# One trunk kernel: the score sweep on row tiles, with unpadded queries, and output squares read from PSUM

## The reference, cut to what matters

```python
rel = b[:, :, :, :, None, :] - b[:, :, :, None, :, :]        # b: cumulated log decay
pair_decay = jnp.exp(jnp.minimum(rel, 0.0)) * causal[:, :, None]
scores = jnp.einsum('bhnid,bhnjd,bhnijd->bhnij', qc, kc, pair_decay)
o_intra = jnp.einsum('bhnij,bhnjv->bhniv', scores, vc)
...
o = rms_norm(o, out_norm) * jax.nn.silu(r.reshape(B, S, H, GLA_DV))
```

## Time and profile before

| | us |
|---|---|
| median of three runs (1468.25 to 1469.93) | 1468.33 |
| the profiled execution | 1469.45 |
| its span | 1467.7 |
| PE busy | 1432.9 (98%) |
| weight loads busy | 1175.7 (80%) |
| DVE, ACT, POOL busy | 727.6, 618.6, 651.1 |
| mean granted TensorE clock | 0.994 |

### The profile page before, as it was taken

One profiled execution on the slowest core, in us unless ns is written; L12 is line 12 of the kernel. 1 busy time (PEld: TensorE's weight loads), 2 busy tenths in 40 slices (PEclk: granted clock), 3 DMA queues, 4 the chain that ended last, 5 costly groups with the idle time before them and its releaser, 6 DMA issues.

```text
span 1467.7 us, 17267 instructions
## 1 busy us (share of the span) xinstructions
PE 1432.9 (98%) x6777; PEld 1175.7 (80%) x6777; DVE 727.6 (50%) x1122; ACT 618.6 (42%) x1073; POOL 651.1 (44%) x369
## 2 busy tenths in 40 slices
PE   8999989999999999999999999999999999999999
PEld 6878778886888888888878776878867888888887
DVE  6473585244566404663135645843536663166621
ACT  5646572465432212232246455735644322222221
POOL 4646253452344434444346354624524344444442
PEclk9999999999999999999999999999999999999999
DMA  6322002331233232332333310123312333333322
GB/s 166 105 88 71 16 3 88 99 114 58 75 98 102 92 108 87 102 99 94 88 86 91 97 59 15 50 66 101 110 48 83 105 90 104 93 100 90 107 85 93
DMA packets 174208, 125.66 MB, mean 86 GB/s; under 512 B 12561, under 2 KB 150576, under 8 KB 174128
## 3 DMA queue, kind: packets, MB, share of 16 engines
q1 hardware_dynamic: 173568, 124.55, 28.3%
q10 hardware_dynamic: 560, 0.01, 0.0%
HBM read 122.44 MB, written 2.10 MB: 85 GB/s over the span
## 4 chain that ended last, share of the span: by engine, by line
PE 91%; DVE 5%; ACT 2%; POOL 1%; issue 1%; DMA 1%; SPq 0%; DVEq 0%
PE bank L608 26%; PE bank L610 26%; PE bank L609 26%; PE bank L871 3%; PE bank L718 1%; PE bank L616 1%; PE bank L830 1%; PE bank L831 1%; PE bank L706 1%; DVE h L1494 1%; ACT cprobs L1084 1%; DMA h<-in_x 1%; POOL scores_h L473 1%; DVE state L1666 1%; PE bank L775 0%
## 5 line engine op out<-in xcount | busy, mean ns | idle before, releaser
L535 POOL TENSOR_TENSOR w_lo<-raw,w_hi 128x1024 fp32r<-128x1024 f32 (+1 forms) x230 | 543.6, 2367 | 735.1 <-ACT w_hi L1045 735.0
L1045 ACT ACTIVATE w_hi<-raw 128x1024 fp32r<-128x1024 f32 (+1 forms) x230 | 237.6, 1036 | 337.1 <-PE bank L610 333.6
L608 PE MATMUL bank<-x_hi,w_hi 128*128 128x512 f32 (+1 forms) x880 | 345.0, 392 | 0.7 <-issue 0.7
L609 PE MATMUL bank<-x_lo,w_hi 128*128 128x512 f32 (+1 forms) x880 | 342.9, 390 | 0.0
L610 PE MATMUL bank<-x_hi,w_lo 128*128 128x512 f32 (+1 forms) x880 | 342.9, 390 | 0.0
L608 PEld LDWEIGHTS bank<-x_hi,w_hi 128*128 128x128 f32 (+1 forms) x880 | 165.0, 187 | 38.1 <-issue 3.4
L609 PEld LDWEIGHTS bank<-x_lo,w_hi 128*128 128x128 f32 (+1 forms) x880 | 164.9, 187 | 35.3 <-issue 0.8
L610 PEld LDWEIGHTS bank<-x_hi,w_lo 128*128 128x128 f32 (+1 forms) x880 | 164.8, 187 | 35.4
L1494 DVE TENSOR_TENSOR h<-h,bank 128x512 f32<-128x512 f32 x64 | 43.7, 688 | 223.9 <-PE bank L610 223.9
L608 PE MATMUL bank<-w_hi,a_hi 128*128 128x512 f32 x352 | 137.0, 389 | 0.0
L610 PE MATMUL bank<-w_hi,a_lo 128*128 128x512 f32 x352 | 136.9, 389 | 0.0
(11 more groups left out here) (288 smaller groups left out, 2100.2 us busy)
## 6 DMA issues: line engine op xcount, KB each, us to landing
raw<-in_w_ffn_in SPq DMA_DIRECT2D x88, 512.0 KB, 3.8
raw<-in_w_ffn_out SPq DMA_DIRECT2D x40, 512.0 KB, 3.7
raw<-in_w_in SPq DMA_DIRECT2D x28, 512.0 KB, 3.8
raw<-in_w_mix_out SPq DMA_DIRECT2D x16, 512.0 KB, 3.8
raw<-in_w_ca_kv SPq DMA_DIRECT2D x32, 256.0 KB, 3.3
raw<-in_w_in SPq DMA_DIRECT2D x18, 256.0 KB, 3.0
raw<-in_w_ca_q SPq DMA_DIRECT2D x8, 512.0 KB, 3.7
raw<-in_w_ca_out SPq DMA_DIRECT2D x8, 512.0 KB, 3.9
```

The lines of the kernel that those rows point to most:

```text
L535: pool.tensor_tensor(w_lo[gi % SPLIT][:, 0:n], raw[gi % RAW][:, 0:n], w_hi[gi % SPLIT][:, 0:n].bitcast(f32), ALU.subtract).then_inc(S["lo_ ...
L608: pe.matmul(o, ah, bh, start=first, stop=False)
L609: pe.matmul(o, ah, bl, start=False, stop=False)
L1045: act_.activation(w_hi[k % SPLIT][:, 0:n], raw[k % RAW][:, 0:n], ACT.Copy).then_inc(S["hi_split"], 1)
```

## The change

The queries are read from `Q` itself; `Qx`, its zeros, `expand` and ACT's part in the sweep are gone. A head's matmul uses only the partitions of that head (32 or 64 rows of the array), and two heads on different rows are issued in turns, into two banks. For x = 0 there are two parts, heads 0 and 1, then heads 2 and 3 into the other half of the same two banks; PE waits on its own semaphore `row_pair` between them. Keys are not cut by block any more. All levels have the same 32 matmuls of 64 moving columns and 128 stationary columns.

```diff
+                    def level(x, m, f, r, bank, c):
+                        dk = HDK if x else GDK
+                        rows_ = slice(dk * r, dk * (r + 1))
+                        for n in range(NT):
+                            q = Q[rows_, f, n * P:(n + 1) * P].rearrange("p (c two m) -> p c two m", two=2, m=m)
+                            yield pe.matmul(pb[bank][:, c + 64 * n:c + 64 * (n + 1)].rearrange("p (c m) -> p c m", m=m),
+                                            K[rows_, f, n * P:(n + 1) * P], q[:, :, 1, :], start=True, stop=True)
...
-                            pe.wait_ge(S["qx_done"], past(layer, "qx_done") + 2 * li + x + 1)
+                            pe.wait_ge(S["q_level"], past(layer, "q_level") + 2 * li + x + 1)
                             if li:
                                 pe.wait_ge(S["k_level"], past(layer, "k_level") + 2 * (li - 1) + x + 1)
+                                pe.wait_ge(S["swept"], past(layer, "swept") + 2 * (li - 1) + x + 1)
+                                if li > MASKED_LEVELS:
+                                    pe.wait_ge(S["swept_a"], past(layer, "swept_a") + 2 * (li - 1 - MASKED_LEVELS) + x + 1)
...
+                            for part in range(2):
+                                if x == 0:
+                                    if part:
+                                        pe.wait_ge(S["row_pair"], past(layer, "row_pair") + 2 * (li + 1))
+                                    for mm0, mm1 in zip(level(0, m, 0, 2 * part, 0, 256 * part), level(0, m, 0, 2 * part + 1, 1, 256 * part)):
+                                        pass
...
+                                else:
+                                    for mm0, mm1 in zip(level(1, m, 1 + part, 0, 2, 256 * part), level(1, m, 1 + part, 1, 3, 256 * part)):
+                                        pass
```

DVE updates a mixer's queries only after that mixer's matmuls of the level (they read `Q` now), and then copies. At the two largest block sizes (m = 32, 64; `MASKED_LEVELS = 5`) it copies one bank a mixer, and ACT the other, without a mask, by blocks of keys:

```diff
                     for li, m in enumerate(LEVELS):
...
+                        for x, sc in enumerate((scores_g, scores_h)):
+                            dve.wait_ge(S["sweep_mm"], past(layer, "sweep_mm") + 4 * li + 2 * (x + 1))
                             next_queries(x, m)
+                            for r in range(2 if li < MASKED_LEVELS else 1):
...
+                                ins = dve.copy_predicated(odd_blocks(pair, m), mask, found)
+                            ins.then_inc(S["swept"], 1)
```

```diff
-                pool.wait_ge(S["tok_mm"], past(layer, "tok_mm") + 2 * NT)
-                score_base(pool, 1)
-                pool.wait_ge(S["pv_mm"], past(layer, "pv_mm") + NH)
-                for x in range(2):
-                    pool.memset(Qx[x][1][:, :, :], 0.0).then_inc(S["zeroed"], 1)
-                pool.memset(state[:, :, :], 0.0).then_inc(S["zeroed"], 1)
```

For the outputs, ACT squares `o` straight from PSUM into one of two buffers; DVE sums one tile ahead, multiplies straight from PSUM, and frees the bank itself:

```diff
+                            act_.activation(o_sq[:, n % 2, :], pb[O_BANKS[n]][:, :], ACT.Square).then_inc(S["o_sq_done"], 1)
...
+                    squares(0)
+                    for n in range(NT):
+                        if n + 1 < NT:
+                            squares(n + 1)
+                        gated(n)
```

More of the change, by code:

```diff
@@ L563, in _ @@
                         if i == slab_at["cig", 3]:
-                            first_query_zeros(pool, layer)
+                            score_bases(pool, layer)
                         if i == slab_at["mix", 0, 1]:
@@ L854, in _ @@
                     for li, m in enumerate(LEVELS):
                         for x in range(2):
-                            pe.wait_ge(S["qx_done"], past(layer, "qx_done") + 2 * li + x + 1)
+                            pe.wait_ge(S["q_level"], past(layer, "q_level") + 2 * li + x + 1)
                             if li:
                                 pe.wait_ge(S["k_level"], past(layer, "k_level") + 2 * (li - 1) + x + 1)
[L859 to L872, removed]
-                                if n % 2:
-                                    mark(mm, S["sweep_mm"])
-                                    freed[b] = (S["swept"], past(layer, "swept") + 4 * li + b + 1)
@@ L876, in _ @@
+                            mm0.then_inc(S["sweep_mm"], 1)
+                            mm1.then_inc(S["sweep_mm"], 1)
                         if li:
                             mix_units("sweep")
+                    for b in range(4):
+                        freed[b] = (S["swept"], past(layer, "swept") + 2 * len(LEVELS))
+                    pe.wait_ge(S["swept_a"], past(layer, "swept_a") + 2 * (len(LEVELS) - MASKED_LEVELS))
                     pe.wait_ge(S["k_level"], past(layer, "k_level") + 2 * len(LEVELS))
@@ L1273, in _ @@
                     act_.preload_act_table_set(LOG_EXP)
+                    for li in range(MASKED_LEVELS, len(LEVELS)):
+                        m = LEVELS[li]
+                        for x, sc in enumerate((scores_g, scores_h)):
+                            act_.wait_ge(S["sweep_mm"], past(layer, "sweep_mm") + 4 * li + 2 * (x + 1))
+                            found = pb[2 * x + 1][:, :].rearrange("p (f b m) -> p f b m", f=2, m=m)
+                            pair = odd_blocks(sc[:, 2:4].rearrange("p f n q -> p f (n q)"), m)
+                            n_c = P // (2 * m)
+                            for c in range(n_c):
+                                keys = slice(2 * m * c, 2 * m * c + m)
+                                ev = act_.activation(pair[keys, :, c::n_c, :], found[keys, :, c::n_c, :], ACT.Copy)
+                            ev.then_inc(S["swept_a"], 1)
                     for f in range(3):
@@ L1277, in _ @@
                     ahead(("mix", 0, 1))
-                    for n in range(NT):
-                        act_.wait_ge(S["o_mm"], past(layer, "o_mm") + n + 1)
-                        act_.activation(o_tok[:, n, :], pb[O_BANKS[n]][:, :], ACT.Copy).then_inc(S["o_evac"], 1)
-                        c = R_O + 8 * n
-                        act_.wait_ge(S["o_ss"], past(layer, "o_ss") + n + 1)
-                        inverse_rms(small[:, c + 64:c + 72], small[:, c + 32:c + 40], small[:, c:c + 8], GDV, S["o_r"])
+                    for n in range(NT + 1):
+                        if n < NT:
+                            act_.wait_ge(S["o_mm"], past(layer, "o_mm") + n + 1)
+                            if n > 1:
+                                act_.wait_ge(S["o_ss"], past(layer, "o_ss") + n - 1)
+                            act_.activation(o_sq[:, n % 2, :], pb[O_BANKS[n]][:, :], ACT.Square).then_inc(S["o_sq_done"], 1)
+                        if n:
+                            c = R_O + 8 * (n - 1)
+                            act_.wait_ge(S["o_ss"], past(layer, "o_ss") + n)
+                            inverse_rms(small[:, c + 64:c + 72], small[:, c + 32:c + 40], small[:, c:c + 8], GDV, S["o_r"])
                     for c in range(4):
```

125 lines of the change are left out of this document (52 added, 73 removed).

## The result

| | before | after |
|---|---|---|
| median us (4 runs each) | 1468.39 | 1542.43 |
| lowest to highest | 1468.25 to 1469.93 | 1541.47 to 1544.52 |
| profiled execution: span | 1467.7 | 1542.6 |
| mean granted clock | 0.994 | 0.957 |

What follows compares the result with a forecast made beforehand. PE, 91% of the chain of waits, was taken as the bound; +2.7 - 1.8 (layer 0) and +3.9 - 1.8 - 1.2 (layer 1) gave +1.8, so 1470 us, own range 1466 to 1474, 8 in 10 1460 to 1488.

Steps and rivals of the forecast that it cites:

- The clock I take as full; the gaps are under 1 us.: PE in the sweep: full granted clock assumed, since before it fell after a gap of 4.05 us.
- clock stays low: Rival, chance 0.10: gaps before level 2 and short matmuls keep PE at 1.2 GHz; 1479, whole sweep +40.
- my 38.05: Predicted length in us of the layer 1 sweep, level 0 to transposed keys, against 34.13 before.
- The level's own price: PE in a level: 2.08 for x = 0, 1.71 for x = 1, joints 0.18 + 0.15, projection unit 0.89.
- the step over `row_pair`: PE's wait for its own matmuls between the parts of x = 0: 0.36 us more, bounds 0.1 and 0.6.
- my 5.0: PE's predicted us for a middle level with its projection unit, against 4.2 at levels 2 to 4.
- Levels 0 and 1 by DVE: Early sweep: DVE's copies and updates, 5.6 to 5.9 us a level at m = 1 and 2, delay PE.
- The outputs: PE's wait for DVE before the output transposes falls from 2.88 to 1.1 us: -1.8 a layer.
- the -1.2 for the clock: Layer 1 outputs: 1.2 us won back from the 6.3 us stretch at 0.73 clock behind the wait.
- At nothing: 0 to +1: POOL's diagonal multiplies, slab split, wider mask, ACT's copies and SP's loads hide beside other work: 0 to +1 together.

Runs made afterwards that it cites:

- e2: The changed kernel with one output projection unit moved from behind the transposed keys to behind level 0: 1540.64 us, ratio 1.0487.
- e8: The changed kernel with x = 1 matmuls over all 128 partitions, x = 0 still on 32-row tiles: 1584.91 us, ratio 1.0783.
- e1: The changed kernel with all score matmuls of the sweep over 128 partitions, heads not kept apart: 1533.2 us, ratio 1.0432.
- e11: The changed kernel with the two heads of a pair issued one after the other, not in turns: 1577.37 us, ratio 1.0739.
- e9: The kernel before with only the output part of the change: 1464.45 us, ratio 0.9974.
- e4: The kernel before with 64 bytes a partition more ahead of the arena (block for temporaries): 1491.86 us, ratio 1.0154.
- e7: The changed kernel with x = 0 matmuls over all 128 partitions, x = 1 still on 64-row tiles: 1585.59 us, ratio 1.0787.
- e10: The kernel before with the output part and an earlier first key update, padded queries kept: 1458.94 us, ratio 0.993.
- e5: The changed kernel with 192 bytes a partition more ahead of the arena (block for temporaries): 1522.73 us, ratio 1.0362.
- e6: The kernel before with 64 bytes a partition more ahead of all buffers, weights too: 1469.97 us, ratio 0.9999.

## Why the prediction was wrong, point by point

- **The step that failed** is "The clock I take as full; the gaps are under 1 us." It read a gap of 4.05 us ahead of the fall as what a fall needs. The runs show in its place that matmuls on row tiles bring the fall with PE busy: e2, e8 and layer 1 of the change have the fall with no gap, e1 has no fall in the same program on full rows, and the clock then stands at 0.50 for 61.4 us a layer. The rival "clock stays low" named short matmuls on part of the array, but its main case had two levels at the low clock, 1479. For both whole sweeps it gave +40. Measured are 61.23 a sweep against my 38.05, which is +46 for both, and some 2 us a layer for the transposed keys and the unit behind them, still at 0.53.
- **The level's own price was right, at full clock.** Level 0 took, by the starts of its records, 2.24 for x = 0 and 1.73 for x = 1, or 3.97 in all (predicted 2.08 + 1.71 + 0.18). That it agrees so well is partly luck: the step over `row_pair` took 0.363 from start to start, which is 0.25 more than a usual step, where my term was 0.36 more; the usual step was 0.112 and not 0.107, and the first of each part of x = 0 0.16. Two loads on two row tiles run at once: pairs of records start 7 ns apart, every 112 ns. That agrees with the Trainium skill, "TensorEngine Tiling (Array Packing)", section Key Properties. Its section Theoretical Speedup gives up to 2x for a tiling factor of 2: level 0 took 7.53 on full rows in e1 and 4.24 in the change, 1.8 times, which agrees. The gain went into the matmuls that unpadded queries need (64 loads for 24), so against before a level wins nothing. Its 4x for 32 rows was not tried, since never more than two tiles work at once. e11's 112 ns for a load on one row tile alone, against 105 over the full array, bears out the page "TensorE: Matmul & The Clock Gate" of the Trainium skill, section LDWEIGHTS.
- At half clock all but the step over `row_pair` (0.51) takes about twice as long: a pair every 213 ns, a unit 1.57, from one level to the next 210.07 - 200.91 = 9.16 against my 5.0.
- **Levels 0 and 1 by DVE: right in kind, 0.9 us short.** PE waited 1.84 for the first copy. In the timelines of DVE and POOL, the query and the key update start together, and DVE's takes 1.07, where I had 0.42. The difference, 0.65, is most of POOL's 0.84; "SBUF — State Buffer" in the Trainium skill, section "SBUF: two separate sides", has one of the two wait for the whole of the other, and this agrees in the main:

```profile
188.19 1.07 DVE L1630 TENSOR_TENSOR Q<-Q,decay 128x256 f32<-128x256 f32 x1 [1.05 <-PE bank L856]
189.19 2.46 DVE L1652 COPY_PREDICATED scores_g<-pair_mask,bank 128x512 f32<-128x512 uint8 x2
```

```profile
188.14 0.84 POOL L490 TENSOR_TENSOR K<-K,decay 128x256 f32<-128x256 f32 x1 [8.40 <-PE bank L856]
```

- **The outputs: right.** The wait fell by 2.0 (predicted 1.8) in each layer, and the half clock behind it in layer 1 was not there in e9 (1.00). e9 gives -4.2 for both layers, predicted -4.8; the -1.2 for the clock rested on a stretch that comes and goes.
- **"At nothing: 0 to +1" missed the addresses.** The instructions listed there did hide (the mask's cast took 2.02, not 1.6, in a wait of 4.48 that shrank to 2.92). But a buffer removed and one grown moved the arena, and e4 puts +23 on that alone. It was outside my range by itself, and no row of before could have shown it; the two lines of the diff that change the sizes ahead of the arena could.
- Together: 1470 + 46 + 4 for the clock, + 20 for the address is 1540, measured 1542.4. The last 2 us are not assigned.

**Open:** what it is in a matmul on part of the rows that lets the clock fall. Column tiles over all rows (m = 32) did not do it, but stood for only 2 us. Every run with row tiles also changes the tile size two or three times a level, and e1 never; no run separates the two. Against the changes as such stand m = 32 and 64 of before, four changes in 7 us at full clock, but those are of columns. Open too are 64 rows by themselves, one row tile with no second beside it, and why short matmuls on full rows hold a high clock (e1) and don't bring back a low one (e7). And which two operands meet badly when the distance is not 128 modulo 256: weights and arena operands are loaded and streamed in both roles here.

## What to carry to other kernels

A short matmul (here 64 columns) on fewer rows of the array is not priced by its records alone: look at the granted clock over the whole stretch, and try the full-row form, even zero-padded, beside it. Where a tuned kernel gains or loses a buffer, fix the addresses of the rest, or measure the old code with the new layout before judging the change. Take the removable wait first by moving work (e10), and rewrite the inner loop only if something is left.

## What the runs showed of the hardware that was not expected

- Sweeps with matmuls of 64 columns on row tiles, of both sizes or of 32 rows alone, issued in turns or in sequence, had the clock fall to 0.50 with no gap in PE's work and stay there for 61 to 82 us a layer, PE 97 to 99% busy; the same matmuls all over 128 rows had 1.00 (the change, e1, e2, e8, e11).
- With the clock at 0.50, 8.5 us of full-row records in a row, 32 of the 35 with 64 columns, did not raise it (e7).
- The place of one operand's buffer against another's, modulo 256 bytes, is worth 2 to 6 ns on each 512-column matmul of 227 ns: +23 us (e4), -20 us (e5), 0 when all move together (e6).
